# Row normalization moved into the projection that follows it, with turning and scaling in one TensorE product

## The reference

```python
def rmsnorm(x, g):
    y = x * lax.rsqrt(jnp.mean(x * x, axis=-1, keepdims=True) + EPS)
    return y * g
...
q = rmsnorm(h, norm_mem_g) @ w_mq                 # 1024 x 1024
...
u, _ = causal_dwconv(rmsnorm(h, norm_ffn_g) @ w_up, ...)   # 1024 x 5632
h = h + (silu(u_gate) * u_value) @ w_down
```

## Time and profile before

| | us |
|---|---|
| median of three runs | 2290.56 |
| profiled execution, whole | 2293.16 |
| its span on the chip | 2291.9 |
| PE busy in the span | 1994.5 (87%) |
| DVE busy | 1054.5 (46%) |
| ACT busy | 658.2 (29%) |
| POOL busy | 534.5 (23%) |

### The profile page before, as it was taken

One profiled execution on the slowest core, in us unless ns is written; L12 is line 12 of the kernel. 1 busy time (PEld: TensorE's weight loads), 2 busy tenths in 40 slices (PEclk: granted clock), 3 DMA queues, 4 the chain that ended last, 5 costly groups with the idle time before them and its releaser, 6 DMA issues. The chain is left out here.

```text
span 2291.9 us, 28375 instructions
## 1 busy us (share of the span) xinstructions
PE 1994.5 (87%) x10881; PEld 1822.9 (80%) x10881; DVE 1054.5 (46%) x1340; ACT 658.2 (29%) x1198; POOL 534.5 (23%) x459
## 2 busy tenths in 40 slices
PE   3999999465974689669999698999999999999997
PEld 3999999254863578559988586999999999999996
DVE  4222444486444321151124113465757575756666
ACT  4112222433442331431140122422222323232322
POOL 3000000133321150520020151223323232332320
PEclk9999999776886789879999899999999999999999
DMA  3222210210112030421013310111011111111012
GB/s 112 60 75 71 58 49 21 63 37 14 33 45 105 1 129 1 147 89 40 1 74 129 127 40 28 47 28 55 27 55 36 47 43 40 53 30 55 27 37 90
DMA packets 122324, 127.00 MB, mean 55 GB/s; under 512 B 10261, under 2 KB 104574, under 8 KB 121950
## 3 DMA queue, kind: packets, MB, share of 16 engines
q1 hardware_dynamic: 117630, 120.89, 17.1%
q10 hardware_dynamic: 3714, 4.76, 0.7%
q0 software_dynamic: 896, 0.19, 0.0%
HBM read 109.86 MB, written 15.96 MB: 55 GB/s over the span
## 5 line engine op out<-in xcount | busy, mean ns | idle before, releaser
L2574 PE MATMUL ffn_banks<-h_hi,up_hi 128*128 128x384 f32 x1056 | 353.6, 335 | 1.8 <-PEq L116 1.8
L2574 PE MATMUL ffn_banks<-h_hi,up_lo 128*128 128x384 f32 x1056 | 353.5, 335 | 0.0
L2574 PE MATMUL ffn_banks<-h_lo,up_hi 128*128 128x384 f32 x1056 | 353.4, 335 | 0.0
L2749 DVE TENSOR_TENSOR h<-h,ffn_banks 128x512 f32<-128x512 f32 x396 | 272.2, 688 | 146.3 <-PE ffn_banks L2609 142.0
L2719 DVE SCALAR_TENSOR_TENSOR ffn_conv_out<-ffn_conv_in,vec,ffn_conv_out 128x1168 f32<-128x1168 f32 x88 | 206.7, 2348 | 129.8 <-ACT ffn_conv_out L2640 124.1
L549 PE MATMUL proj_banks<-x_hi,in_w_hi 128*128 128x384 f32 (+1 forms) x648 | 218.6, 337 | 0.0
L549 PE MATMUL proj_banks<-x_lo,in_w_hi 128*128 128x384 f32 (+1 forms) x648 | 217.3, 335 | 0.0
L549 PE MATMUL proj_banks<-x_hi,in_w_lo 128*128 128x384 f32 (+1 forms) x648 | 217.2, 335 | 0.0
L2574 PEld LDWEIGHTS ffn_banks<-h_hi,up_hi 128*128 128x128 f32 x1056 | 198.8, 188 | 2.9 <-issue 2.0
L2574 PEld LDWEIGHTS ffn_banks<-h_lo,up_hi 128*128 128x128 f32 x1056 | 198.7, 188 | 0.9
L2574 PEld LDWEIGHTS ffn_banks<-h_hi,up_lo 128*128 128x128 f32 x1056 | 198.6, 188 | 0.0
(11 more groups left out here) (409 smaller groups left out, 3594.9 us busy)
## 6 DMA issues: line engine op xcount, KB each, us to landing
up_raw<-in_w_up SPq DMA_DIRECT2D x44, 512.0 KB, 6.0
in_w_raw<-in_w_in SPq DMA_DIRECT2D x22, 512.0 KB, 4.3
down_raw<-in_w_down SPq DMA_DIRECT2D x22, 512.0 KB, 3.6
mem_k_one<-in_cache_mem_k SPq DMA_DIRECT2D x8, 1024.0 KB, 5.1
spill<-mixT SPq DMA_DIRECT2D x10, 576.0 KB, 5.3
wo_w_raw<-in_w_o SPq DMA_DIRECT2D x8, 512.0 KB, 3.6
h<-in_x_prompt SPq DMA_DIRECT2D x8, 512.0 KB, 7.6
mkv_w_raw<-in_w_mk SPq DMA_DIRECT2D x8, 512.0 KB, 3.9
```

The source lines that it names most:

```text
L2574: ins = nc.tensor.matmul(banks[:, NP * s + p, 0:TC], wt[:, s, k, :], x[:, k, TC * p:TC * p + TC], start=(n == 0), stop=(n == 3 * KD - 1))
L2749: nc.vector.tensor_tensor(to, to, banks[:, d_bank[n % 5], :], ALU.add).then_inc(added, 1)
```

## The change

Both phases `norm_turn` are gone for `h` (the first one of the kernel, `nx`, and that of the memory, `nm`, stay). Their work is done by a new class `NormParts` inside the block of the projection:

- ACT takes all 9 roots at once (`factors`), DVE inverts them and writes 9 diagonal matrices of 128 x 128, the identity times the inverse lengths (`scale`). The row tiles themselves are no longer scaled.
- PE forms `h` tile (stationary) times diagonal (moving) as an ordinary product of fp32 operands in place of a transpose (`turn`): turned and scaled in one. 72 of them.
- ACT and DVE write `hi` and `lo` as before, 24 instructions each, ring of 4 banks.
- PE runs 8 parts ahead of its first product, and the other 16 between the products of the first weight tile (`before_product`), which stands behind the unchanged wait for `split`.
- `hi` of the first two weight tiles is made by ACT, the first ahead of the 24 `hi` parts, the second behind them (`high_first`); POOL makes only `lo` (`low_parts`, `low_first`). In the query projection POOL makes `lo` of all 8 weight tiles, not DVE.

```diff
--- before.py
+++ after.py
@@ -376,6 +376,82 @@
+class NormParts:
+    GROUP, RING = 3, 4
+    def __init__(self, nc, C, ph, tag, src, sums, gain_col, hi, lo, xn, banks):
+        self.nc, self.C, self.src, self.sums, self.gain_col = nc, C, src, sums, gain_col
+        self.hi, self.lo, self.banks = hi, lo, banks
+        self.diagonal = xn[:, 0:NT * P].rearrange("p (t c) -> p t c", t=NT)
+        self.root, self.inv = (ph.sb(f"{tag}_{n}", [P, NT]) for n in ("root", "inv"))
+        self.rooted, self.inverted, self.scaled, self.turned, self.high, self.low = (
+            ph.sem(f"{tag}_{n}") for n in ("rooted", "inverted", "scaled", "turned", "high", "low"))
+    def factors(self):
+        self.nc.scalar.activation(self.root[:], self.sums[:], ACT.Sqrt, scale=1.0 / D, bias=self.C.eps[:, 0:1]
+                                  ).then_inc(self.rooted, 1)
+    def inverse(self, dve):
+        dve.wait_ge(self.rooted, 1)
+        self.nc.vector.reciprocal(self.inv[:], self.root[:]).then_inc(self.inverted, 1)
+        dve.wait_ge(self.inverted, 1)
+    def scale(self, g):
+        for j in range(self.GROUP):
+            t = g * self.GROUP + j
+            self.nc.vector.tensor_scalar(self.diagonal[:, t, :], self.C.ident[:], self.inv[:, t:t + 1], None, ALU.mult
+                                         ).then_inc(self.scaled, 1)
+    def part(self, i):
+        g, k = divmod(i, KD)
+        return k, slice(g * TC, g * TC + TC), self.banks[i % self.RING][:, 0:TC], self.C.vec[:, self.gain_col + k:self.gain_col + k + 1]
+    def turn(self, pe, i):
+        g, k = divmod(i, KD)
+        pe.wait_ge(self.scaled, self.GROUP * (g + 1))
+        if i >= self.RING:
+            pe.wait_ge(self.low, i - self.RING + 1)
+        for j in range(self.GROUP):
+            t = g * self.GROUP + j
+            ins = self.nc.tensor.matmul(self.banks[i % self.RING][:, j * P:j * P + P], self.src[:, t, k * P:k * P + P],
+                                        self.diagonal[:, t, :], start=True, stop=True)
+        ins.then_inc(self.turned, 1)
+    def high_part(self, act, i):
+        k, cols, bank, gain = self.part(i)
+        act.wait_ge(self.turned, i + 1)
+        self.nc.scalar.activation(self.hi[:, k, cols], bank, ACT.Copy, scale=gain).then_inc(self.high, 1)
+    def low_part(self, dve, i):
+        k, cols, bank, gain = self.part(i)
+        dve.wait_ge(self.high, i + 1)
+        self.nc.vector.scalar_tensor_tensor(self.lo[:, k, cols], bank, gain, self.hi[:, k, cols].bitcast(F32), ALU.mult,
+                                            ALU.subtract).then_inc(self.low, 1)
+    def on_scalar(self, act):
+        for i in range(NP * KD):
+            self.high_part(act, i)
+    def on_vector(self, dve):
+        self.inverse(dve)
+        for g in range(NP):
+            self.scale(g)
+        for i in range(NP * KD):
+            self.low_part(dve, i)
+    def before_product(self, pe, p, k):
+        if p == 0 and k == 0:
+            for i in range(KD):
+                self.turn(pe, i)
+        i = KD * p + k + KD // 2
+        if KD <= i < NP * KD:
+            self.turn(pe, i)
+        pe.wait_ge(self.low, KD * p + k + 1)
 class FeatureWeights:
@@ -399,6 +475,16 @@
     def load_first(self, sp):
         for n in range(self.RING):
             self.load(sp, n)
+    def high_first(self, nc, act, n):
+        self.wait(act, n)
+        nc.scalar.activation(self.hi[:, n], self.raw[:, n], ACT.Copy).then_inc(self.high, 1)
+    def low_parts(self, nc, pool, n_tiles):
+        for n in range(n_tiles):
+            pool.wait_ge(self.high, n + 1)
+            nc.gpsimd.tensor_tensor(self.lo[:, n % 2], self.raw[:, n % self.RING], self.hi[:, n % 2].bitcast(F32), ALU.subtract
+                                    ).then_inc(self.split, 1)
     def split_first(self, nc, pool):
         for n in range(2):
@@ -2155,7 +2241,7 @@
                 nc.vector.tensor_tensor(to, to, banks[:, n % 8, :], ALU.add).then_inc(freed, 1)
-def query_projection(nc, C, tag, hi, lo, weights, n_tiles, out, inv_norm):
+def query_projection(nc, C, tag, src, src_sums, gain_col, hi, lo, weights, n_tiles, out, inv_norm):
     RING = weights.RING
@@ -2165,15 +2251,24 @@
         squares = ph.sb(f"{tag}_squares", [P, 2, T])
         root = ph.sb(f"{tag}_root", [P, NT, HEADS])
         sums = ph.psum(f"{tag}_sums", [P, NT, HEADS])
+        more = ph.psum(f"{tag}_more", [P, 512])
+        norm = NormParts(nc, C, ph, f"{tag}_norm", src, src_sums, gain_col, hi, lo,
+                         out[:].rearrange("p k t -> p (k t)")[:, KD * T - 6 * D:KD * T],
+                         [banks[:, NP + p, :] for p in range(NP)] + [more[:]])
         projected, freed, squared, summed, rooted, inverted = (ph.sem(f"{tag}_{n}") for n in (
             "projected", "freed", "squared", "summed", "rooted", "inverted"))
         block = ph.block()
         @block.sync
         def _(sp):
+            weights.load_first(sp)
             for n in range(RING, n_tiles):
                 sp.wait_ge(split, n - RING + 1)
                 weights.load(sp, n)
+        @block.gpsimd
+        def _(pool):
+            weights.low_parts(nc, pool, n_tiles)
         @block.tensor
         def _(pe):
@@ -2191,6 +2286,8 @@
                     pe.wait_ge(freed, n - 1)
                 for p in range(NP):
                     for k in range(KD):
+                        if n == 0:
+                            norm.before_product(pe, p, k)
                         for i, (w, x) in enumerate(((w_hi, hi), (w_hi, lo), (w_lo, hi))):
                             ins = nc.tensor.matmul(banks[:, (n % 2) * NP + p, 0:TC], w[:, n % 2, k, :],
                                                    x[:, k, TC * p:TC * p + TC], start=(k == 0 and i == 0),
@@ -2208,6 +2305,10 @@
                     act.wait_ge(projected, NP * (n - 1))
                 nc.scalar.activation(w_hi[:, n % 2], weights.raw[:, n % RING], ACT.Copy).then_inc(high, 1)
+            norm.factors()
+            weights.high_first(nc, act, 0)
+            norm.on_scalar(act)
+            weights.high_first(nc, act, 1)
             for n in range(n_tiles):
                 for p in range(NP):
                     act.wait_ge(projected, NP * n + p + 1)
@@ -2220,11 +2321,8 @@
         @block.vector
         def _(dve):
+            norm.on_vector(dve)
             for n in range(n_tiles):
-                if n + 2 < n_tiles:
-                    dve.wait_ge(high, n + 3)
-                    nc.vector.tensor_tensor(w_lo[:, n % 2], weights.raw[:, n % RING], w_hi[:, n % 2].bitcast(F32),
-                                            ALU.subtract).then_inc(split, 1)
                 dve.wait_ge(freed, n + 1)
                 if n >= 2:
                     dve.wait_ge(summed, n - 1)
@@ -2463,10 +2561,12 @@
     def load_down(self, sp, f):
         sp.dma_start(self.d_raw[:], self.w_down[bass.ds(P * f, P), :]).then_inc(self.d_landed, 16)
-    def split_first(self, nc, pool):
+    def high_first(self, nc, act, s):
+        act.wait_ge(self.w_landed[s], 16)
+        nc.scalar.activation(self.hi[:, s], self.raw[:, s], ACT.Copy).then_inc(self.high[s], 1)
+    def low_first(self, nc, pool):
         for s in range(2):
-            pool.wait_ge(self.w_landed[s], 16)
-            nc.gpsimd.tensor_copy(self.hi[:, s], self.raw[:, s]).then_inc(self.high[s], 1)
             pool.wait_ge(self.high[s], 1)
             nc.gpsimd.tensor_tensor(self.lo[:, s], self.raw[:, s], self.hi[:, s].bitcast(F32), ALU.subtract
                                     ).then_inc(self.split[s], 1)
@@ -2491,11 +2591,14 @@
         w_hi, w_lo, w_high, split = weights.hi, weights.lo, weights.high, weights.split
         d_hi, d_lo = ph.sb("down_hi", [P, D], F32R), ph.sb("down_lo", [P, D], F32R)
         xp = ph.sb("ffn_conv_in", [P, 2, L])
-        y = ph.sb("ffn_conv_out", [P, 2, LY + 2])
+        room = ph.sb("ffn_room", [P, 6 * D])
+        y = room[:, 0:2 * (LY + 2)].rearrange("p (s c) -> p s c", s=2)
         a = ph.sb("ffn_gated", [P, T])
         a_hi, a_lo = ph.sb("gated_hi", [P, T], F32R), ph.sb("gated_lo", [P, T], F32R)
         tails = ph.sb("ffn_tails", [P, 2, NF, 18])
         banks = ph.psum("ffn_banks", [P, 8, 512])
+        norm = NormParts(nc, C, ph, "nf", h, C.h_sums, V_FFN, hi, lo, room[:],
+                         [banks[:, n, :] for n in (3, 4, 5, 7)])
         d_bank = (2, 6, 7, 0, 1)
@@ -2570,6 +2675,8 @@
                 for p in range(NP):
                     n = 0
                     for k in range(KD):
+                        if s == G and not before:
+                            norm.before_product(pe, p, k)
                         for wt, x in ((w_hi, hi), (w_hi, lo), (w_lo, hi)):
                             ins = nc.tensor.matmul(banks[:, NP * s + p, 0:TC], wt[:, s, k, :], x[:, k, TC * p:TC * p + TC],
                                                    start=(n == 0), stop=(n == 3 * KD - 1))
@@ -2673,6 +2784,7 @@
         @block.gpsimd
         def _(pool):
```

(7 more changed lines are left out.)

## The result

The changed kernel takes 2302.87 us (median of 10 runs, 2298.87 to 2307.63), the kernel before on the same chip 2292.01 (10 runs, 2287.35 to 2296.76). The ratio is 1.0045, with a 95% interval of 1.0033 to 1.0056: slower by 10.9 us. The forecast was 10.7 us more on the profiled execution and 2302.0 us in all, in a range of 2296 to 2311.

What follows compares the result with a forecast made beforehand. PE, busy 87% of the span, was taken as the bound; start, turning, clock, changing and second-tile terms made query 6.7 and feed-forward 4.0 us later, together 10.7, forecast 2302.0 us, range 2296 to 2311.

Steps and rivals of the forecast that it cites:

- Part 1: Start of turning in both stages: PE waits for the first weight tile's split, starting at 1012.5 and 1425.9 us.
- Part 2: Turning on PE: three fp32 diagonal products take 0.67 us in place of 0.33, 24 parts 16.1 us a stage.
- rival (b): Turned product costs PE one record, like a transpose: 8.0 us less per stage, not slower, 2288 us; chance 0.07.
- Part 3: PE's clock after idling: turning starts at 1.2 GHz for 4.0 us, 2.0 us lost in each stage.
- Rival (a): Clock falls in the pause before the second weight tile: 1.6 to 2.3 us lost per stage, 2305.5 us; chance 0.23.
- The weighing of that rival: Skill's rule says the pause before the second weight tile costs no clock; an earlier feed-forward pause suggested 1.5 us per stage.
- part 5: Second weight tile: its hi stands behind all 24 hi parts on ACT, so PE waits 1.7 us in each stage.
- the argument that the prediction had against (a): Before the earlier feed-forward pause PE had thin work at DVE's pace; before the new pause work will be dense.
- Part 4: Interleaved turning and projection: 16 changes from fp32 to fp32r products cost PE 0.09 us each, 1.4 in each stage.
- rival (c): Small terms at their low ends, clock 1.4 and no changing cost: 6.7 us later, 2297.5 us, within 0.3%; chance 0.13.

Runs made afterwards that it cites:

- feed-forward-only kernel: The change made in the feed-forward stage alone, the query stage left as in the kernel before; 2297.02 us, ratio 1.0017 to the kernel before.
- query-only kernel: The change made in the query stage alone, the feed-forward stage left as in the kernel before; 2299.26 us, ratio 1.0021 to the kernel before.

## Why the prediction was right

The time came out as forecast, and so did the mechanism: the start behind the weights, the second record, the clock at the start and the late second weight tile. One term of the sum, the cost of going to and fro, is not there. The terms, each with its working against what the profile after shows, in us; "start" is from the stage's root to PE's first turned product:

| term | query, predicted | measured | feed-forward, predicted | measured |
|---|---|---|---|---|
| start | 8.4 | 10.1 | 7.0 | 6.7 |
| first 8 parts, clock in it | 7.4 | 7.4 | 7.4 | 8.0 |
| first weight tile with 16 parts | 24.6 | 23.4 | 24.6 | 23.4 |
| pause before the second | 1.7 | 1.6 | 1.7 | 1.6 |
| sum | 42.1 | 42.4 | 40.7 | 39.7 |
| more than before | 6.7 | 7.0 | 4.0 | 2.9 |

Measured are, in the query stage, 1013.60 - 1003.54, 1020.98 - 1013.60, 1044.37 - 1020.98 (the last product starts at 1044.20 and takes its pitch of 0.17) and 1045.97 - 1044.37; the other stage likewise from its rows. The second weight tile came 35.4 and 36.7 us after the root in the kernel before, as the prediction's sum had it.

**Part 1, the start: right in its cause, 1.7 us short in the query stage.** PE waits for POOL in both stages, as said, and nothing else of the new work is on that way. ACT's 1.06 and POOL's 2.34 are those of the prediction. The term that was off is the weights' landing, which I took over from the earlier trace rows as a fixed time: there from issue 1005.04 to POOL's copy at 1008.94, 3.9 us; in the profile after from 1004.49 to 1010.07, 5.6. The issue stands at the same distance from the root in both (0.95 us). Over the nine profiles in which nothing else holds the engine that waits for this tile it is 3.9 to 5.7 us, and 4.95 in the feed-forward-only kernel, whose query stage is that of the kernel before. So the 3.9 was the low end of a spread that one profile can't show.

**Part 2, the turned product is two records: right.** Line 418 in the query stage, PE's groups by form:

```profile
L418 PE MATMUL mq_banks<-mem_q_t,h 128*128 128x128 f32 x108 | 16.3, 300 | 11.1 <-POOL mq_w_lo L486 11.1
...
L418 PE MATMUL mq_more<-mem_q_t,h 128*128 128x128 f32 x36 | 5.1, 278 | 0.0
```

108 + 36 = 144 records for 72 products. This is rival (b) refuted, by its own row; and transposes in the same place won 7.7 and 7.9 us, about the 8.0 that the second record was priced at. The 1.3 us that rival (b) gave back for DVE's pace did not show. The Trainium skill ("FP8 and Floating Point Precision", section "TensorE Precision Notes") puts true fp32 at several passes through the array; the records and the doubled time agree in direction, but a count of passes is not seen in the trace.

**Part 3, the clock: right, and shown apart.** 2.0 lost in the query stage (7.38 less 8 x 0.67) where 2.0 stood, and 2.6 in the feed-forward stage. With PE kept busy in the wait, 2.1 and 2.6 came back. Rival (a), a fall of the clock behind the pause, did not come: the window 1463.00:1466.00 has 1.00 across the pause.

The weighing of that rival took one pause of the kernel before for the rule, and there are two. The query stage has the same pause, 1.76 us, behind the same 36 transposes, and its products ran at 1.00. The experiments show both outcomes again with that code: in the feed-forward-only kernel the query's first products got 0.55 behind a pause of 1.87 us, in the query-only kernel the feed-forward products got 1.00 behind 1.75:

```profile
1451.87:1454.87 3.00, 3.00 (x17) 3.00 (x18) 0.00 (x0) 0.00 (x0) 0.26 (x2) 1.00 0.44 120
```

So the clock fell in two of four such cases. In the 3 us of transposes that end 1.7 us ahead of the first product it was 0.84 and 0.74 where it then fell, and 1.00 and 0.95 where it held. Behind the pause of part 5, ahead of which PE works without a gap at 1.00, it fell in none of fourteen cases in eight profiles. This fits the argument that the prediction had against (a), but no run varied what stands ahead of a pause, so the cause stays open. The Trainium skill ("TensorE: Matmul & The Clock Gate", section "Why this matters for your kernels") warns only of longer gaps; the fourteen pauses agree with it, and the two of 1.75 and 1.87 us behind which the clock fell don't.

**Part 4, going to and fro: this step was wrong.** It put 1.4 us in each stage for 16 changes from fp32 to fp32r products. The stretch has 16 x 1.193 us, which is 0.67 + 0.52, the two kinds of work side by side with nothing added; the whole first weight tile is 23.4 where 12.5 + 16 x 0.67 = 23.2. The 0.09 that I read out of the earlier trace rows is there (1023.76 to 1024.02 is 0.26). But the six records of a part take only 0.59 from their first start to the next product's (1023.17 to 1023.76), 0.08 under 0.67. I had counted the longer gap behind a change and not the shorter one at it. 2.8 us too much in all; of the low ends that made rival (c), this one came true. That the total is nevertheless so near is in part luck: the late weights of the query stage (1.7) and the clock of the feed-forward stage (0.6) took most of its place, the two stages came out 0.7 under the forecast, and 0.4 us from code that did not change brought the two profiles to 10.4 apart.

**Part 5, the second weight tile: right.** 1.60 and 1.59 us, with 1.7 forecast, and the edit that moves its `hi` takes them away. That POOL makes `lo` of the later query tiles costs nothing: the two waits shown are the only ones of PE for line 486 in the query stage.

**The end.** The 0.83 us from the first drain of V on are code that did not change. In all the profiles this stretch lies between 831.9 and 833.7 us, so I give no cause for it.

## What to carry to other kernels

Folding a scale into a transpose as a product with a diagonal is no free ride where the operands are fp32: it took 0.67 us for three tiles where transposes take 0.335, and here it moved load from an engine with half of its time idle to the one that bounds the kernel. When preparation is moved into the block of its consumer, look first at where the old wait stands: the turning needed no weights, and putting it ahead of that wait was worth 12 us. The doubled work costs nothing where PE would wait anyway, and its full price where PE is the bound. Before taking work off an idle engine, ask what that work costs now; scaled rows and transposes, in the new order, gave the best kernel (2278 us).

## What the hardware showed that was not expected

- Changing between fp32 and fp32r products in PE's stream costs nothing that adds up: a period of 1.193 us for 0.67 + 0.52 of work.
- A weight tile of 512 KB, issued at the same point of the program, was taken up 3.9 us after its issue in one profile and 5.6 in another, with 3.9 to 5.7 over nine profiles. An estimate made with one such duration is good to some 2 us where PE waits for it.
- The 18 one-column fp32 products that sum the squares of the last query tile took 4.30 us in the changed kernel and 6.13 in that changed in the query stage only, by the same code. The rows of both, and the windows behind their starts (clock 1.00 and 0.68):

```profile
1145.52 4.30 PE L2279 MATMUL mq_sums<-ones,mq_squares 128*128 128x1 f32 x36
```

```profile
1145.50:1150.00 4.50, 4.25 (x38) 4.08 (x36) 1.36 (x1) 0.63 (x2) 0.00 (x0) 1.00 0.00 0
```

```profile
1144.95 6.13 PE L2279 MATMUL mq_sums<-ones,mq_squares 128*128 128x1 f32 x36
```

```profile
1145.50:1150.00 4.50, 4.43 (x28) 4.34 (x27) 1.36 (x1) 0.14 (x1) 0.00 (x0) 0.68 0.00 0
```

PE was at work on weights in nearly all of both stretches, and the clock was not the same. What decides it stays open.

- Behind the same code and nearly the same pause (1.75 to 1.87 us) the clock held at 2.4 GHz in two cases and fell to 1.2 GHz in two, one of each in either stage. One observed pause gives no rule.
